# Forgetting layer: a pair's third dense piece moved in front of the pair's transposes

## The reference

```python
proj = (h @ w_in).astype(jnp.float32)
q, k, v, g, fl = jnp.split(proj, [FOX_WIDTH, 2 * FOX_WIDTH, 3 * FOX_WIDTH, 4 * FOX_WIDTH], axis=-1)
...
cumf = jnp.cumsum(jax.nn.log_sigmoid(fl + b_f), axis=1).transpose(0, 2, 1)
for blk in range(s_ // FOX_BLOCK):          # 4 blocks of 128 queries
    logits = q_blk @ k[:q1].T * scale + cumf[q] - cumf[k]     # causal, 16 heads of 64
    outs.append(softmax(logits) @ v[:q1])
o = concat(outs) * jax.nn.silu(g)
return o @ w_out
```

## Time and profile before

| | us |
|---|---|
| median of 3 runs (1705.78 to 1706.29) | 1705.82 |
| the profiled execution, its own device time | 1707.55 |
| its span, first to last instruction | 1705.8 |
| PE busy in the span | 1687.0 (99%) |
| pairs 0 to 7 of the forgetting layer | about 1536 to 1658 of the span |
| output product behind them | 1658 to 1702 |

### The profile page before, as it was taken

One profiled execution on the slowest core, in us unless ns is written; L12 is line 12 of the kernel. 1 busy time (PEld: TensorE's weight loads), 2 busy tenths in 40 slices (PEclk: granted clock), 3 DMA queues, 4 the chain that ended last, 5 costly groups with the idle time before them and its releaser, 6 DMA issues.

```text
span 1705.8 us, 25667 instructions
## 1 busy us (share of the span) xinstructions
PE 1687.0 (99%) x9753; PEld 1396.9 (82%) x9753; DVE 1040.8 (61%) x1717; ACT 759.3 (45%) x1332; POOL 807.7 (47%) x617
## 2 busy tenths in 40 slices
PE   9999999999999999999999999999999999999999
PEld 7777788888888888888888888887877888887887
DVE  5887567555564872664475555678377844237752
ACT  4443644222222354664532222234544457666650
POOL 6635236555555473232465555553532335453342
PEclk9999999999999999999999999999999999999999
DMA  9735237444445243222274444442322133334522
GB/s 369 253 138 201 84 124 271 173 170 164 163 158 194 99 136 112 87 83 92 98 272 173 172 172 172 172 165 82 99 75 69 51 100 100 106 89 129 160 89 74
DMA packets 114833, 242.72 MB, mean 142 GB/s; under 512 B 6144, under 2 KB 27776, under 8 KB 114736
## 3 DMA queue, kind: packets, MB, share of 16 engines
q1 hardware_dynamic: 112560, 237.20, 40.3%
q10 hardware_dynamic: 2176, 4.19, 0.8%
HBM read 239.21 MB, written 2.16 MB: 141 GB/s over the span
## 4 chain that ended last, share of the span: by engine, by line
PE 87%; DVE 6%; DMA 2%; ACT 2%; issue 1%; POOL 1%; SPq 0%; DVEq 0%; POOLq 0%; ACTq 0%
PE bank L242 40%; PE bank L656 20%; PE bank L1674 5%; PE bank L1640 3%; PE bank L453 3%; PE bank L432 2%; PE bank L1642 2%; DMA ct<-cumd 1%; PE bank L1758 1%; PE bank L416 1%; PE bank L1722 1%; PE bank L1234 1%; PE bank L1746 1%; PE bank L2253 1%; DVE fP L1850 1%
## 5 line engine op out<-in xcount | busy, mean ns | idle before, releaser
L2755 POOL TENSOR_TENSOR wsp<-raw,wsp 128x512 fp32r<-128x512 f32 x516 | 761.7, 1508 | 803.4 <-ACT wsp L197 803.4
L242 PE MATMUL bank<-xT,wsp 128*128 128x512 f32 x2016 | 464.9, 390 | 0.0
L242 PEld LDWEIGHTS bank<-xT,wsp 128*128 128x128 f32 x2016 | 377.7, 188 | 80.0 <-issue 0.9
L197 ACT ACTIVATE wsp<-raw 128x1024 fp32r<-128x1024 f32 x131 | 138.8, 1060 | 464.0 <-PE bank L656 240.3
L656 PE MATMUL bank<-wsp,hT 128*128 128x512 f32 x1344 | 308.2, 389 | 0.0
L242 PE MATMUL bank<-wsp,xT 128*128 128x512 f32 x1248 | 299.9, 396 | 1.3 <-DVE tok L2519 0.9
L656 PEld LDWEIGHTS bank<-wsp,hT 128*128 128x128 f32 x1344 | 252.3, 188 | 52.4
L242 PEld LDWEIGHTS bank<-wsp,xT 128*128 128x128 f32 x1248 | 231.8, 189 | 54.8 <-issue 4.8
L874 DVE CUSTOM_DVE_ANT_0 ada_ring<-ada_ring,crow,cols 128x1024 f32<-128x1024 f32 x96 | 148.4, 1580 | 4.5 <-DMA ada_ring<-in_ada_rows 4.5
L200 ACT ACTIVATE wsp<-raw 128x1024 fp32r<-128x1024 f32 x131 | 137.2, 1047 | 0.0
L795 DVE TENSOR_TENSOR x<-bank,x 128x512 f32<-128x512 f32 x80 | 55.2, 690 | 110.5 <-PE bank L656 110.5
(11 more groups left out here) (351 smaller groups left out, 2161.1 us busy)
## 6 DMA issues: line engine op xcount, KB each, us to landing
raw<-in_ff_w SPq DMA_DIRECT2D x64, 1024.0 KB, 5.2
ada_ring<-in_ada_rows SPq DMA_DIRECT2D x96, 512.0 KB, 6.3
tok<-in_ada_rows SPq DMA_DIRECT2D x32, 512.0 KB, 5.5
raw<-in_odd_w_in SPq DMA_DIRECT2D x16, 1024.0 KB, 5.4
raw<-in_gla_w_in SPq DMA_DIRECT2D x12, 1024.0 KB, 7.2
raw<-in_att_w_in SPq DMA_DIRECT2D x12, 1024.0 KB, 5.2
raw<-in_even_w_in SPq DMA_DIRECT2D x12, 1024.0 KB, 5.2
ring_s<-in_ada_rows SPq DMA_DIRECT2D x16, 512.0 KB, 11.0
```

Of the source, the lines that this page charges most:

```text
L197: act.activation(home[:, 0, 0:HK // 2], raw[:, slot, 0:HK // 2], ACT.Copy).then_inc(hi_part, 1)
L242: mm = pe.matmul(out_ap, l, r, start=(start and a == b), stop=(stop and a == 1))
L2755: ins = pool.tensor_tensor(w[:, 1, k], raw[:, slot, k], w[:, 0, k].bitcast(F32), ALU.subtract)
```

## The change

In the pairs without a quarter as third piece, and only in the call without `ahead` (the forgetting layer), `dense(u + 2)` is issued before the four groups of transposes and no longer behind them. `dense(u + 3)` stays where it was. No instruction is added or taken away, and no wait condition is edited.

```diff
                 quarters = u + 2 in work and work[u + 2][6] - work[u + 2][5] == KT // ST
+                before = not quarters and not ahead
+                if before:
+                    dense(u + 2)
                 for w in range(u, u + ST):
                     if w == u + 3 and quarters:
                         dense(u + 2)
                     turned(w)
-                if not quarters:
+                if not quarters and not before:
                     dense(u + 2)
                 dense(u + 3)
```

## The result

The changed kernel takes 1712.76 us (median of 6 runs, 1711.19 to 1714.33) against 1705.80 (6 runs, 1705.11 to 1706.29): a ratio of 1.0039, 95% interval 1.0029 to 1.0049, so 7.0 us slower. The forecast was 1710.0, with a range of 1708.6 to 1712.6; the median lies 0.2 us above the range.

A forecast was written before the change was run, and what follows sets the result against it. PE, busy 99% of the span, was taken as the bound. Shifts of +1.36, +0.83 and +1.41 us brought PE into pair 7 at +3.60; the end came at +4.2, so 1705.82 + 4.2 = 1710.0 us, range 1708.6 to 1712.6.

The forecast's parts named there:

- The bound and the possible gain: PE busy 99% of the span; its idle time at the transposes, 1.44 us or 0.08%, is all the move could win.
- The wait that travels with the piece: Pairs 1, 3, 5, 7: third piece waits for its bank's last reader, PE idle 1.9, 0.8, 1.4, 2.0 us.
- The transposes at 1.40 us a pair: Pairs 1, 3, 5, 7: the 40 transposes run after the third piece and add 1.40 us each.
- The pieces at 5.66 and 5.94 us: Third and fourth pieces together keep their old length: 5.66 us for gate pieces (pair 1), 5.94 for value pieces (pair 3).
- The delay swallowed in pair 7: PE enters pair 7 at +3.60; 0.75 us goes into old idle time, so the third piece comes at +2.85.
- No fall of the clock: The forecast assumes the clock stays at 1.00 in the new idle stretches; chance 0.50.
- The rival with one fall: New idle time lowers PE's clock once, costing 1.7 us: 1711.7 us; chance 0.25.
- Copies at nothing: ACT's copies of the transposes cost nothing: the piece behind covers them; otherwise at most about 1 us in a pair.
- The masked bias of pair 7: Rival: pair 7's maxima hang on the masked bias alone, shifting 2.2 not 2.9 us; end +3.5, 1709.3 us; chance 0.09.
- The filled gap: Rival: bank free when second piece ends, idle 0.30 and 1.14 us won: 1704.4 us; chance 0.06 together with unchanged time.
- the unchanged time: Rival: ready transposes pass the waiting piece, so nothing changes: 1705.8 us; chance 0.06 together with the filled gap.

The follow-up runs named there:

- the last run: Kernel before, plus ACT copying gate tiles to SBUF to free the bank, and third piece between second and third transpose groups in pairs 0, 1, 2, 7: ratio 0.9992.
- the early copy in the old order: Kernel before, with ACT copying each gate tile to SBUF to free the bank, tanh and DVE's multiply reading the copy: ratio 1.0001, +0.5 us.
- the early copy in the changed order: Changed kernel, with ACT copying each gate tile to SBUF to free the bank sooner: ratio 1.0016, +2.8 us against the kernel before.

## Why the prediction was right, and where it was short

*The bound and the possible gain.* Right: PE's waits for line 1859 in pairs 1 and 7 went away, as foreseen, and no gain came of it.

*The wait that travels with the piece.* Right in place and cause, and in size but for pair 7: the waits were 1.76, 0.75, 1.41 and 2.42 us, in front of the lines named and ended by the engines named (forecast 1.9, 0.8, 1.4, 2.0). The run with the bank freed sooner shows that they come from the bank: the waits shrink with it, and so does the loss.

*The transposes at 1.40 us a pair.* Right: 1.41, 1.40, 1.40, 1.40. Leaving only 16 of them behind the piece brought the loss from 5.5 us without the fall to 2.25.

*The pieces at 5.66 and 5.94 us.* Too small. A run of 24 matmuls cut in two by the transposes took 2.95 + 2.94 us in pair 1, and two value pieces of 24 took 3.07 + 3.06 in pair 3. Left in one run, behind the same kind of wait, the 48 matmuls of pair 3 took 5.94 us with both pieces in front, so the cut is what costs. Pairs 1, 3 and 5 cost 1.57, 1.01 and 1.59 us (forecast 1.36, 0.83 and 1.41): 0.57 us in the three, and 0.23 more in pair 7.

*The delay swallowed in pair 7.* Partly wrong. Not 0.75 us but 0.33 was swallowed: PE entered pair 7 at +4.17, and the third piece came at +3.84, not +2.85. Of the 0.99 us of difference, 0.57 is the delay brought along. The other 0.42 goes with the remainder subtraction, which took 1.27 us and not 0.80, so that the maxima started at 1643.99, +3.90 counted from the start of the pairs.

*No fall of the clock.* This is the step that failed: "My forecast without a fall of the clock". In pair 7 of the profiled execution the clock fell and cost 1.6 us (forecast for one fall 1.7), and the run with pair 7 alone shows the same behind 2.45 us. With it the terms close: 4.24 by the forecast's sum, 0.57 brought along, 0.42 in pair 7, 0.23 for its cut run and 1.60 for the clock make 7.06 of the 7.07. Without the fall the change would have cost 5.5 us by the same lengths, which is 1711.3 and inside the range. The rival with one fall, 1711.7, was nearer than the forecast, and it is that rival's place in the range that brought its upper end within 0.2 us of the median. In the other three pairs the clock stayed at 1.00 in the changed kernel. Which of the 6 timed runs had a fall can't be seen run by run; that their 3.1 us of spread are falls in some of them and not in others, here or in the first layer, is likely, not shown.

*Copies at nothing.* Right: no wait of lines 1718, 1722 or 1758 in the changed kernel; with both pieces in front there is one, of 0.5 us.

*The other rivals.* The masked bias of pair 7 did come at +2.2, counted from the start of the pairs, as that rival has it and not at the forecast's +2.56, but it wasn't last: the maxima followed the remainder subtraction. The filled gap and the unchanged time are excluded by the waits. In the last run, the gap was filled and the pairs were 1.88 us shorter in the profile, once the bank was free in time and the piece stood behind the first 24 transposes. That fits the point named for that rival, the release of the bank.

## What to carry to other kernels

Before filler work is moved forward to close a gap, look up what it waits for itself: here one accumulation bank made each new tile wait for the readers of the last, and ready transposes were held behind that wait. Moving one piece away from its neighbour also cut a run of matmuls in two, which cost 0.2 us each time here, and a new wait of 2.4 us lowered TensorE's clock, which cost 1.6 us on top. Look whether the resource can be freed first, and count what freeing it costs.

## What the hardware showed that wasn't expected

Idle times of like length had different consequences. In pair 1 the clock stayed at 1.00 after 1.76, 1.81 and 1.68 us in three executions and fell after 1.80 in a fourth; in pair 7 it fell after 1.96, 2.42 and 2.45 us, and stayed after 1.15. The first layer's wait is 1.66 or 1.67 us long in seven of the ten profiles: the clock fell behind it in four (the kernel before, pair 1 only, the early copy in the old order, the last run) and stayed at 1.00 in three (pair 7 only, the early copy in the changed order, both pieces in front). So the length of the wait alone doesn't decide, and what does stays open. A fall cost 1.6 to 1.7 us each time, the same for 12 matmuls (4.55 for 2.95) as for 24 (7.3 for 5.66).

DVE's remainder subtraction on two SBUF operands takes 0.69 us where POOL is idle, and took 1.27 and 1.53 us in pair 7 of the two executions above in which it ran beside POOL's subtractions; POOL's four (line 2758) then took 5.47 and 5.48 us where they take 5.03 in the kernel before, behind pair 1:

```profile
1565.47 5.03 POOL L2755 TENSOR_TENSOR wsp<-raw,wsp 128x512 fp32r<-128x512 f32 x4
...
1565.96 0.69 DVE L2141 SCALAR_TENSOR_TENSOR gT<-gT,bank 128x512 f32<-128x512 f32 x1 [2.15 <-ACT gT L2079]
```

The second row is the gate multiply beside the same POOL work: with one operand in a PSUM bank it took 0.69 us. With the early copy both of its operands lie in SBUF, and at the same place in the changed order it took 1.75, with POOL's four at 5.91. The Trainium skill, SBUF — State Buffer, section "SBUF: two separate sides", says that VectorE with two SBUF inputs and GpSimd take turns on one port pair, whole instructions at a time; these rows agree. It is the likely reason why the maxima of pair 7 came some 0.4 us later than forecast; no run here takes POOL's work away to show it.
